# A hybrid decoder layer on eight cores: channel mixers cut by d_ff, and three tiles of them scheduled inside the token mixers

## The chip, the cores and the metric

One Trainium2 chip; the program runs on all 8 of its cores at once, each core on its own batch element, with no traffic between them. The metric is the device time of one execution, in microseconds (us), of the slowest core. Lower is better.

## The reference, cut to what matters

```python
def reference(x, mem, positions, ...):
    h = x                                                    # (8, 2048, 1024)
    h = h + 0.5 * _swiglu(_rmsnorm(h, ffn1_norm), wg1, wu1, wd1)    # D_FF = 2816
    h = h + _mixer(h, mem, positions, ...)
    h = h + 0.5 * _swiglu(_rmsnorm(h, ffn2_norm), wg2, wu2, wd2)
    return _rmsnorm(h, final_norm)

def _swiglu(x, wg, wu, wd):
    return (jax.nn.silu(x @ wg) * (x @ wu)) @ wd

def _mixer(...):
    z = _rmsnorm(h, mix_norm) @ w_in        # cq, ckv, krope, gq, gk, gv, ga, gr, xq, gz
    o_mla = _mla(...) @ mla_w_o             # 8 heads, causal, over all earlier tokens
    o_gla = _gla(...) @ gla_w_o             # 4 heads, a state carried along the sequence
    o_x = _cross(...) @ x_w_o               # 4 heads into 256 memory tokens
    gates = jax.nn.sigmoid(gz + gate_bias)  # three gates per channel
    return (gates[0] * o_mla + gates[1] * o_gla + gates[2] * o_x) @ w_out
```

The two `_swiglu` are the channel mixers, `_mixer` is the token mixer. The channel mixers work on each token alone; the token mixer of a token needs the tokens before it.

## The kernel before, in words

The 2048 tokens of a core are four tiles of 512 tokens (TT). Everything is kept transposed, channels on the 128 partitions and tokens along the free axis, so a matmul is 128x128 weights against 128x512 activations and fills one of the eight PSUM banks. All four tiles of the residual h lie in SBUF (`hS`, 4 x 8 pieces of 128x512 f32).

The program is written as a list of operations (`FW.add`), each with the engines that may run it, a cost, and its dependences from the tiles it reads and writes. `FW.schedule` (L172) then plays the list through: it keeps a clock for each engine, takes the operation that can start first, and among those that are ready on an engine the one that was written down first. The result is a fixed order on each engine; `emit` writes it out with semaphore waits. Which PSUM bank and which weight slot an operation uses is settled when it is written down, before the order is known: `bank` (L401) and `pair` (L407) go round fixed sets (PA banks 0 to 3 for attention scores, bank 4 for attention outputs, PQ banks 5 to 7 for the rest of the token mixer), and `slot_view` (L493) goes round six weight slots (`ring`) of 128x2048 bf16.

The stages stand one behind the other:

- Norm and first channel mixer for all four tiles (`ffn`, L601). It goes over d_ff in 11 groups of 256. For a group it loads three slots of weights (`wload`, L498: f32 in DRAM, cast to bf16 on the way, issued from GpSimd's queue), and for each tile does 4 banks of 8 matmuls for gate and up rows, then Silu on ScalarE and a product on VectorE; then `down` (L604) does 8 banks of 2 matmuls, and VectorE adds each bank to h, so h is read and written once per group and channel piece. Beside it `side1` (L985) issues small work: constants, rope tables, keys and values of the memory (`memory_kv`), and the conversion of the token mixer's 42 weight blocks from f32 to bf16 in DRAM (`convert`, L505, five per group, also from GpSimd's queue, which it shares with `wload`).
- Four token mixers, tile after tile (`mixer_tile`, L685): projections; attention over all tiles so far (the scores of two key blocks in a pair of banks, one Exp of 128x1024); between heads two "units" of the linear attention and cross attention (`fill`); then the merge, 12 steps of a gate projection (slot wz, 16 matmuls) and an output projection (slot wo, 8 matmuls); then w_out. Its weights come by `mload` (L509) from the bf16 copy, on SyncE's queue.
- Norm and second channel mixer for all four tiles, the final norm (`done2`, L1023), and the store.

The softmax here doesn't subtract the row's maximum and nothing guards it: scores larger than these inputs give would overflow.

## Time and profile before

| | us |
|---|---|
| three timed runs | 1950.38, 1957.6, 2092.74 |
| their median | 1957.6 |
| the profiled execution: span of the slowest core | 1966.7 |
| spans of its eight cores | 1937.1 to 1966.7 |
| TensorE (PE) busy in it | 1725.2 (88%) |
| VectorE (DVE) busy | 1014.5 (52%) |
| ScalarE (ACT) busy | 669.7 (34%) |

The profile follows one execution on its slowest core. Its span runs from the first instruction to the last and is the own time that is known of it; a timed run gives a device time, and the median of these lies 9 us below that span. "PE busy" counts matmuls as they stream; the granted clock (PEclk) says at what part of 2.4 GHz. The DMA share is the mean busy share of the core's 16 DMA engines.

### The profile page before, as it was taken

What the parts mean: (1) busy time and instruction counts of PE and PEld (TensorE: products, weight loads), DVE (VectorE), ACT (ScalarE), POOL (GpSimd) and SP (SyncE); (2) the same over time, 40 slices, a digit from 0 to 9 for tenths busy, and PEclk for the clock granted to TensorE, in tenths of its full rate; (3) what the DMA queues carried; (4) which work ended last, traced back from release to release, by engine and by line L of the source; (5) the groups of instructions that cost most, each with busy time, mean ns of one, the idle gap of its engine ahead of it and who ended that gap; (6) DMA issues with size and microseconds to landing.
All of it is one profiled execution on the core that took longest, in us unless ns stands there. A gap on an engine that the chain in (4) does not pass through costs nothing.

```text
span 1966.7 us, 23970 instructions; the slowest of 8 cores (1937.1 to 1966.7 us)
## 1 busy us (share of the span) xinstructions
PE 1725.2 (88%) x7714; PEld 773.3 (39%) x7868; DVE 1014.5 (52%) x1718; ACT 669.7 (34%) x1014; POOL 60.0 (3%) x119
## 2 busy tenths in 40 slices
PE   2999995999987689867997889968899999999995
PEld 0444443344434234423442334423344444444442
DVE  3767772554555334432444334532348555666567
ACT  3411111001125642556334862658543111111124
POOL 1000001000000000000000000000000000000000
PEclk9999997788989799987998999979999999999998
DMA  9388877245232035600462014312253211122104
GB/s 224 62 101 100 105 108 101 37 59 74 53 126 87 30 97 162 187 26 33 134 222 78 27 61 165 117 33 103 83 143 54 43 33 33 33 50 48 33 1 171
DMA packets 49512, 168.91 MB, mean 86 GB/s; under 512 B 6816, under 2 KB 9264, under 8 KB 48432
## 3 DMA queue, kind: packets, MB, share of 16 engines
q0 software_dynamic: 13424, 55.55, 20.2%
q1 hardware_dynamic: 35968, 111.81, 17.5%
q8 instruction: 69, 1.13, 0.2%
q14 instruction: 51, 0.42, 0.1%
HBM read 204.00 MB, written 35.39 MB: 122 GB/s over the span
## 4 chain that ended last, share of the span: by engine, by line
PE 80%; ACT 7%; DVE 5%; issue 4%; DMA 3%; SPq 0%; ACTq 0%; DVEq 0%; POOLq 0%
PE ps_all L433 80%; ACT sa L459 2%; DMA hS<-x 2%; ACT hS L459 2%; DMA ring<-f 1%; ACT sa L897 1%; DVE hS L471 1%; DVE ntm L471 1%; ACT L459 1%; DVE om L466 1%; DVE sb L466 1%; ACT sa L908 0%; DVE hS L466 0%; DVE og L471 0%; ACT hS L482 0%
## 5 line engine op out<-in xcount | busy, mean ns | idle before, releaser
L433 PE MATMUL ps_all<-B,ring 128*128 128x512 bf16 x2760 | 638.6, 388 | 23.0 <-DMA ring<-f 17.5
L471 DVE SCALAR_TENSOR_TENSOR hS<-ps_all,hS 128x512 f32<-128x512 f32 (+1 forms) x744 | 457.1, 682 | 41.9 <-PE ps_all L433 40.6
L433 PE MATMUL ps_all<-sb,ring 128*128 128x512 bf16 (+1 forms) x1787 | 427.0, 389 | 15.7 <-DVE sb L471 6.1
L433 PEld LDWEIGHTS ps_all<-B,ring 128*128 128x128 bf16 x2816 | 279.9, 100 | 369.2 <-issue 84.3
L459 ACT ACTIVATE sa<-ps_all 128x512 f32<-128x512 f32 (+2 forms) x256 | 145.1, 569 | 790.8 <-PE ps_all L433 758.8
L433 PE MATMUL ps_all<-ntm,ring 128*128 128x512 bf16 x1310 | 328.7, 396 | 32.1 <-DVE ntm L471 11.2
L466 DVE TENSOR_TENSOR sb<-sa,ps_all 128x512 bf16<-128x512 f32 x176 | 120.4, 687 | 361.5 <-PE ps_all L433 354.7
L433 PEld LDWEIGHTS ps_all<-sb,ring 128*128 128x128 bf16 x1824 | 182.5, 100 | 238.0 <-issue 51.4
L433 PEld LDWEIGHTS ps_all<-ntm,ring 128*128 128x128 bf16 x1344 | 133.8, 101 | 203.1 <-issue 63.0
L471 DVE SCALAR_TENSOR_TENSOR sa<-sa,ps_all 128x512 f32<-128x512 f32 x96 | 65.6, 687 | 132.1 <-PE ps_all L433 110.6
L433 PE MATMUL ps_all<-sb,B 128*128 128x512 bf16 (+3 forms) x313 | 91.8, 367 | 34.3 <-ACT sa L897 18.3
L433 PE MATMUL ps_all<-sa,va 128*128 128x512 bf16 (+3 forms) x315 | 104.3, 386 | 19.8 <-DVE om L466 18.8
L459 ACT ACTIVATE sa<-ps_all,hv 128x512 f32<-128x512 f32 x96 | 65.3, 686 | 164.8 <-PE ps_all L433 150.3
L897 ACT ACTIVATE sa<-ps_all 128x1024 bf16<-128x1024 f32 x96 | 95.2, 1022 | 24.2 <-PE ps_all L433 20.3
L459 ACT ACTIVATE sb<-hS 128x512 bf16<-128x512 f32 x128 | 75.0, 623 | 55.6 <-DMA hS<-x 25.6
L433 PE MATMUL ps_all<-sb,ones 128*128 128x512 bf16 (+1 forms) x151 | 52.1, 410 | 44.7 <-ACT sb L459 34.9
L163 POOL DMA_DIRECT2D ring<-f x66 | 35.4, 539 | 1700.3 <-PE ps_all L433 1625.0
L459 ACT ACT_TABLE_LOAD x39 | 50.0, 1283 | 55.8 <-PE ps_all L433 48.1
L466 DVE TENSOR_TENSOR sa<-sa,utri 128x128 bf16<-128x128 bf16 (+1 forms) x96 | 22.6, 246 | 79.5 <-ACT sa L908 49.7
L471 DVE SCALAR_TENSOR_TENSOR B<-hS,vecs_s,sa 128x512 bf16<-128x512 f32 x64 | 43.1, 747 | 34.4 <-ACT sa L459 34.4
L466 DVE TENSOR_TENSOR om<-ps_all,sa 64x512 bf16<-64x512 f32 x32 | 22.0, 687 | 73.9 <-ACT sa L459 64.6
L433 PEld LDWEIGHTS ps_all<-sb,B 128*128 128x128 bf16 x320 | 28.7, 101 | 79.1 <-issue 66.1
(99 smaller groups left out, 973.6 us busy)
## 6 DMA issues: line engine op xcount, KB each, us to landing
ring<-wb SPq DMA_DIRECT2D x112, 512.0 KB, 4.0
ring<-f POOLq DMA_DIRECT2D x66, 512.0 KB, 6.8
wb<-wm POOLq DMA_DIRECT2D x28, 512.0 KB, 17.2
ring<-wb SPq DMA_DIRECT2D x48, 256.0 KB, 3.7
hS<-x SPq DMA_DIRECT2D x16, 512.0 KB, 30.8
spill<-hS SPq DMA_DIRECT2D x4, 2048.0 KB, 8.9
hS<-spill SPq DMA_DIRECT2D x16, 512.0 KB, 5.7
outT<-hS SPq DMA_DIRECT2D x16, 512.0 KB, 2.8
```

Of the source, the lines that this page charges most:

```text
L163: op = self.add([(q, lambda e: e.dma_start(out=o, in_=i), 0.9 if q == "pool" else 0.06)], outs=[out, *outs], ins=[in_, *ins], waits=waits)
L433: i = e.matmul(_ap(o), lhsT=_ap(l), rhs=_ap(r), start=st, stop=sp)
L459: f.add([("act", lambda e: e.activation(out=_ap(out), in_=_ap(in_), func=func, scale=_ap(scale), **kw), c_act(out, bias is not None))], ou ...
L466: f.add([(eng, lambda e: e.tensor_tensor(out=_ap(out), in0=_ap(a), in1=_ap(b), op=op), c_dve(out, rate))], outs=[out], ins=[a, b, *extra_ins])
L471: f.add([("dve", lambda e: e.scalar_tensor_tensor(out=_ap(out), in0=_ap(in0), scalar=_ap(scalar), in1=_ap(in1), op0=op0, op1=op1), c_dve(o ...
L897: f.add([("act", lambda e, PT=PT, ap2=ap2: e.activation(out=PT.bf().ap.rearrange("p (a b) -> p a b", a=2), in_=ap2, func=AF.Exp, scale=SC) ...
```

## The change

What it does, part by part:

1. **Channel mixer, new form.** `ffn` goes over d_ff in parts of 5, 5, 4, 4, 4 blocks of 128 (8, 7, 7 for a single tile). In a part it makes all activations of the part (tiles `aT`), block by block: one slot holds gate and up weights of a block. Then it makes the part's down projection with 4 or 5 (8 or 7) matmuls into one bank, and VectorE adds that bank to h once per part. The matmuls are the same number.
2. **Order of the stages.** The first channel mixer runs for tiles 0, 1, 2 as a stage of its own ("ffn1a"; weights used by three tiles). Tile 3's is written as a stream with its order number raised by LATER (`f.base`), so that the planner takes from it only what no operation of the token mixers can use. The second channel mixer of tiles 0 and 1 are two more such streams. That of tiles 2 and 3 has a base too, but its slots belong to a later epoch, and it runs as the last stage ("ffn2b"). A stream of one tile loads all weights of its channel mixer anew, as f32 with the cast.
3. **Banks and slots bound at issue.** `Bank` objects have a kind; `schedule` gives them a free PSUM bank or one of seven ring slots when their first user is placed, within limits per kind (four banks for a stream, three slots for its weights, four slots for the token mixer's).
4. **Silu in the streams** is Tanh(x/2) and one more VectorE operation.
5. **h leaves SBUF.** There are three places for h tiles in place of four; the token mixer reads h piece by piece from DRAM, adds, writes back (two 256 KB transfers per piece), and the norms before and after read the pieces once more.
6. **Norm sums** of the token mixer's output and of the streams are added up by VectorE, with one matmul at the end in place of eight.
7. **Attention** uses single banks: an Exp of 128x512 per key block in place of one of 128x1024 per two. Copies may go to either engine. The rope rows are spread by two transfers in place of 16 per tile.
8. **Beginning.** x of tile 0 is loaded first, the first weights are tied behind parts of x, and the first 15 tile-blocks have a written order (OPENING). `convert` issues two blocks per 128 of d_ff. x of tile 3 is streamed in for its norm.
9. **The planner's constants**: 270 GB/s in place of 300 for a transfer, 1.6 us (SyncE) or 2.6 us (GpSimd) behind it, a DMA is not issued more than 4 us ahead of the backlog, ScalarE may put off an operation for the sake of the loaded table.

```diff
 class FW:
...
-    def schedule(self):
+    def schedule(self, places, limits):
...
+        def begin_at(op, t):
+
+            for b in op.opens:
+                if not empty[b.store] or not tokens[b.kind] or line[b.kind][-1] is not b or ahead.get(b.epoch - 1):
+                    return None
+                t = max(t, min(empty[b.store])[0], min(tokens[b.kind]))
+            return t
+
+        pri = [op.pri for op in ops]
...
             op = ops[s]
+            for b in op.opens:
+                spot = min(empty[b.store])
+                empty[b.store].remove(spot)
...
+                b.ap = places[b.store][b.place]
+                op.deps.update(spot[2])
...
+SPLIT = (5, 5, 4, 4, 4)
+WIDE = (8, 7, 7)
+NS = max(SPLIT)
+LATER = 1000000
...
+    limits = {"f": 8, "w": 4, "s": 3, "o": 1, "q": 2, "m": 6, "g": 1, "x": 2, "n": 2,
+              "rf": 7, "rw": 3, "rm": 4}
...
+    def ffn(w, xs, hs, kind, silu, landed, side, split=SPLIT, by_tile=False, keep=None, opening=None):
...
+                pg, pu = bank(kind), bank(kind)
+                for p, o in ((pg, 0), (pu, 8)):
+                    for k0 in (0, 4):
+                        mm([(p, wgu[j][:, o + k, :], xs[i][k], k == 0, k == 7) for k in range(k0, k0 + 4)])
+                th = F2.get()
+                if silu:
+                    actf(th, pg, AF.Silu)
+                else:
+                    actf(th, pg, AF.Tanh, scale=0.5)
+                    stt(th, th, 1.0, pg, ALU.add, ALU.mult)
+                tt(a[i][j], th, pu, ALU.mult)
...
+            for q, c2, i in order:
+                c = 2 * q + c2
+                py = bank(kind)
+                for js in (range(ns - 1), (ns - 1,)):
+                    mm([(py, wds[q][:, j, c2 * 128:(c2 + 1) * 128], a[i][j], j == 0, j == ns - 1) for j in js])
+                h = hslot[hs[i]][c]
+                stt(h, py, 0.5 if silu else 0.25, h, ALU.mult, ALU.add)
...
+                py = proj(w_, c2 * 128, 128, mT, bank("m"))
+                hc = M2.get()
+                f.dma("sp", hc, spT[t][c], nbytes=262144)
+                stt(hc, py, 0.5, hc, ALU.mult, ALU.add)
+                f.dma("sp", spT[t][c], hc, nbytes=262144)
+                sums.take(hc)
...
+        if j >= 1:
+            for i in (2 * j - 2, 2 * j - 1):
+                convert(i)
...
+    ffn(f1_d, [nB[0], nB[1], nB[2]], (0, 1, 2), "f", True, lambda i, c: sums[i].take(hslot[i][c]), side1, by_tile=True,
+        opening=OPENING)
...
+    f.base = LATER
+    sums_b = Squares(F2, F1)
+    ffn(f1_d, [nB[3]], (0,), "w", False, lambda i, c: sums_b.take(hslot[0][c]), lambda j: load_x(3, 0) if j == 0 else None, WIDE)
+    f.base = 0
...
+    for t in (0, 1):
+        f.base = (2 + t) * LATER
+        sums_f = Squares(F2, F1)
+        ffn(f2_d, [n2[t]], (t,), "w", False, lambda i, c: sums_f.take(hslot[t][c]),
+            lambda j: reload(t, t) if j == 0 else None, WIDE)
+        final(t, t, sums_f, "w")
```

## Rows read from the trace of the kernel before

**Rows 1.** Stage windows, core 0: busy (count) of PE, PEld, DVE, ACT, POOL; clock, DMA share, GB/s.

```profile
0.00:47.00 47.00, 11.97 (x24) 2.80 (x25) 15.41 (x43) 14.85 (x25) 5.10 (x13) 1.00 0.96 215
47.00:300.00 253.00, 249.00 (x1131) 112.40 (x1152) 185.55 (x307) 51.91 (x83) 21.35 (x42) 1.00 0.74 98
300.00:347.00 47.00, 23.33 (x114) 13.15 (x116) 9.55 (x19) 8.91 (x16) 5.21 (x10) 0.71 0.76 99
347.00:475.00 128.00, 126.98 (x475) 52.91 (x484) 62.80 (x102) 10.75 (x18) 8.31 (x16) 0.81 0.38 50
475.00:561.00 86.00, 85.58 (x389) 38.83 (x395) 49.57 (x81) 10.15 (x17) 2.61 (x5) 0.99 0.34 77
561.00:1457.00 896.00, 742.27 (x3384) 333.58 (x3449) 369.89 (x654) 467.07 (x684) 0.00 (x0) 0.91 0.31 100
1457.00:1920.00 463.00, 459.83 (x2098) 209.12 (x2140) 283.79 (x457) 82.64 (x134) 17.43 (x33) 1.00 0.22 39
1920.00:1967.00 47.00, 26.22 (x111) 10.52 (x110) 37.98 (x59) 23.44 (x37) 0.00 (x0) 0.79 0.45 179
```

**Rows 2.** Windows of core 3, a stretch of the last channel mixer.

```profile
1450.00:1900.00 450.00, 449.93 (x2086) 203.72 (x2085) 277.69 (x450) 73.69 (x118) 14.79 (x28) 1.00 0.21 35
```

**Rows 3.** Waits of the engines, whole span: who for whom, total, times, longest.

```profile
PE ps_all L433 <- DMA ring<-f: 17.5, 1, 17.5
```

**Rows 4.** Timeline of GpSimd's queue before that wait.

```profile
316.82 2.55 POOL L163 DMA_DIRECT2D wb<-wm  x5 [1.20 <-PE ps_all L433]
320.90 1.09 POOL L163 DMA_DIRECT2D ring<-f  x2 [1.53 <-PE ps_all L433]
```

**Rows 5.** Windows in the token mixers: an attention stretch of tile 3, a merge.

```profile
1300.00:1350.00 50.00, 39.45 (x174) 15.67 (x177) 14.59 (x33) 39.91 (x54) 0.00 (x0) 0.88 0.16 54
738.00:800.00 62.00, 59.08 (x281) 27.63 (x285) 25.64 (x38) 19.08 (x29) 0.00 (x0) 1.00 0.64 184
```

**Rows 6.** Waits of PE alone, 580 to 1455 us.

```profile
PE ps_all L433 <- ACT hS L459: 25.7, 24, 1.9
...
PE ps_all L433 <- ACT sa L897: 18.7, 27, 1.8
```

**Rows 7.** DMA, 1457 to 1920 us: a queue's share of 16 engines; issues, KB, us to landing.

```profile
q0 software_dynamic: 4752, 17.30, 21.5%
ring<-f POOLq DMA_DIRECT2D x33, 512.0 KB, 5.2
```

**Rows 8.** The same view, 47 to 347 us.

```profile
q0 software_dynamic: 4791, 25.93, 69.6%
wb<-wm POOLq DMA_DIRECT2D x24, 512.0 KB, 17.4
```

**Rows 9.** The same view, 561 to 1457 us.

```profile
q1 hardware_dynamic: 29423, 88.94, 30.6%
ring<-wb SPq DMA_DIRECT2D x109, 512.0 KB, 4.0
```

**Rows 10.** Groups of instructions on the page: count, busy, mean ns, idle before.

```profile
L471 DVE SCALAR_TENSOR_TENSOR hS<-ps_all,hS 128x512 f32<-128x512 f32 (+1 forms) x744 | 457.1, 682 | 41.9 <-PE ps_all L433 40.6
L897 ACT ACTIVATE sa<-ps_all 128x1024 bf16<-128x1024 f32 x96 | 95.2, 1022 | 24.2 <-PE ps_all L433 20.3
L459 ACT ACTIVATE sa<-ps_all 128x512 f32<-128x512 f32 (+2 forms) x256 | 145.1, 569 | 790.8 <-PE ps_all L433 758.8
```

**Rows 11.** Windows of cores 7 and 3 over one and the same stretch.

```profile
347.00:475.00 128.00, 128.00 (x489) 53.08 (x488) 62.45 (x102) 11.73 (x20) 8.32 (x16) 0.81 0.36 50
347.00:475.00 128.00, 128.00 (x592) 57.95 (x591) 76.00 (x123) 13.75 (x23) 10.93 (x21) 1.00 0.51 67
```

**Rows 12.** Timeline of VectorE: the end of the first norm, and the end of the program.

```profile
28.98 5.39 DVE L471 SCALAR_TENSOR_TENSOR B<-hS,vecs_s,sa 128x512 bf16<-128x512 f32 x8 [19.41 <-ACT sa L459]
1958.10 5.39 DVE L471 SCALAR_TENSOR_TENSOR hS<-hS,vecs_s,sa 128x512 f32<-128x512 f32 x8 [3.41 <-ACT sa L459]
```

More of the change, by code:

```diff
@@ L93, in __init__ @@
         self.marks = []
+        self.base = 0
+        self.loads = 0
+        self.span = 0.0
+        self.busy = {}
         self.handles = {"pe": nc.tensor, "act": nc.scalar, "dve": nc.vector, "pool": nc.gpsimd, "sp": nc.sync}
@@ L145, in add @@
         op.table = table
+        op.pri = self.base + seq
+        for t in {id(_t(x)): _t(x) for x in [*outs, *ins] if isinstance(_t(x), Bank)}.values():
+            if not t.users:
+                op.opens.append(t)
+            t.users.append(seq)
+            op.banks.append(t)
         self.ops.append(op)
@@ L183, in schedule @@
         dma_free = 0.0
-        table = None
+        table = {"none"}
         avail = {e: [] for e in COMPUTE}
@@ L238, in schedule, with emit @@
         self.span = max(op.end for op in ops)
-    def emit(self, outputs):
-        self.schedule()
+        self.busy = {e: sum(next(c for (x, _, c) in o.alts if x == e) for o in ops if o.eng == e) for e in COMPUTE}
+    def emit(self, outputs, places, limits):
+        self.schedule(places, limits)
         sems, counts, known = {}, {}, {}
@@ L702, in mixer_tile @@
+        rmsnorm(kvq[0:3], [vcol(V_QN + i) for i in range(3)], 384, cqn, banks="m")
+        M2.put(*kvq)
+        cp(ga_t, pk[0:16, :])
+        t1, t2, kr = M2.get(), M2.get(), M1.get()
         tt(t1[64:96, :], pk[64:96, :], CS[t][0:32, :], ALU.mult)
@@ L1033, in build_program @@
+    mixer_tile(3, nM[3], lambda: norm_from_dram(2, V_F2, n2[2]), quiet, lambda r: norm_from_dram(3, V_F2, n2[3], r))
+    epoch[0] = 3
+    f.mark("ffn2b")
+    f.base = 4 * LATER
+    sums_l = [Squares(M2, M1, "f") for _ in range(2)]
+    ffn(f2_d, [n2[2], n2[3]], (0, 1), "f", True, lambda i, c: sums_l[i].take(hslot[i][c]),
+        lambda j: [reload(2 + i, i) for i in range(2)] if j == 0 else None, by_tile=True)
+    for i in range(2):
+        final(i, 2 + i, sums_l[i], "f")
     f.mark("end")
-    f.emit(outputs)
+    f.emit(outputs, {"ps": psum, "ring": ring}, limits)
```

785 lines of the change are left out of this document (469 added, 316 removed).

## The prediction

> **What bounds the kernel now.** I read the windows by stage first. Both channel-mixer stages are TensorE streaming without a gap: 459.83 of 463 us busy in the second one at clock 1.00, 249.00 of 253 in the first [rows 1]. The pitch of a 128x512 matmul there is 449.93/2086 = 0.2157 us [rows 2]. Time is lost in five other places [rows 1]. The head: 47 us until the channel mixer starts, with 12 us of PE and DMA at 0.96. A stall in the first mixer: PE is busy 23.33 of 47 us at 300 to 347, the wait behind it is one of 17.5 us on a weight load [rows 3], and GpSimd's queue shows five conversions issued just ahead of two loads [rows 4]. Then 128 us at clock 0.81. The token mixers: 896 us with PE busy 742.27 at a mean clock of 0.91, so 742.27 x 0.91 = 675 us of work at full clock and 221 us lost, a quarter. The tail: 47 us with 26 of PE. In the token mixers no single wait explains the loss: the largest two in PE's own list sum to 44 us and are many short ones on ScalarE [rows 6]; in attention on tile 3 ScalarE is busy 39.91 of 50 us while PE has 39.45 at clock 0.88 [rows 5]. So the stage is a chain of short handovers with too little independent work beside it, and in these stretches the clock is also lower.
>
> **The work that stays.** Matmuls of the channel mixers: 22 blocks x (16 + 8) = 528 per tile and mixer, 8 x 528 = 4224, at 0.2157 us = 911 us, as before. The change can only alter how PE is filled. By stage: three tiles 342 us (1584 matmuls), three streams 342, the last two tiles 228. The token mixers keep 675 us less seven norms whose eight matmuls become one or nothing (7 x 8 x 0.2157 = 12): 663.
>
> **Head.** Before, x of the first tile shares the DMA with the other weights and 6 MB of other x; its norm ends with the eight operations from 28.98 us [rows 12], and the second tile's is waited for too. Now 2.1 MB of x come first; at 215 GB/s [rows 1] that is 10 us, some 3 us to start, and about 5 us of norm before the first eight matmuls flow. I take 18 us, bounds 14 and 29. From there the opening needs 6.3 MB of x and five weight slots while PE has 15 tile-blocks of 16 x 0.2157 = 52 us: 29 us of DMA for x and 5 x 3 to 5 us for the weights fit.
>
> **First stage, three tiles.** 342 us, memory keys and values 9 us, squares 24 x 0.2157 = 5: 356. The risk is DMA. A weight load costs 21.5% x 463 / 33 = 3.0 us of all engines [rows 7]. In the stretch with conversions the queue used 69.6% of 300 us = 209 us [rows 8] for 22 loads (66 us) and the equivalent of 27.5 full conversions, so a conversion costs 5.2 us. The stage needs 33 loads' worth (99), 35.5 full conversions (185), four memory weights (12), x of three tiles (29), tile 3's x twice (19), and some 5 of small things: 349 us of DMA in about 384. That is 91% where before it was 74 to 76% [rows 1], with two conversions of 5.2 us queued per 15.8 us of PE. The seven slots let loads run far ahead, so I take one 10 us stall; bounds 0 and 45 (before, 75% gave about 25 us). VectorE is relieved: h is touched 120 times here in place of once per group, 272 times in the whole program in place of 704 at 0.682 [rows 10], 295 us less. It was hidden behind PE (185.55 of 253 us, 0.73, at most [rows 1]), so it is worth nothing by itself.
>
> **Token mixers with streams.** PE work is 663 + 342 = 1005 us. Three checks that no other resource takes over. ScalarE: 467 us [rows 1], plus 192 single Exps at 0.569 for 96 pairs at 1.022, +11 [rows 10]; one more Exp per head and tile on the diagonal, 32 x 0.2 = 6; streams 66 Tanh and 24 squares at 0.6 = 54: 538, 49% of the stage. VectorE: 370, plus streams 3 x (44 x 0.68 + 24 x 0.68 + 13 x 0.7) = 166, plus norm sums and rereading 45: 581, 53%. DMA: the queue used 30.6% x 896 = 274 us for 88.94 MB, 3.1 us per MB [rows 9]; streams add 99 loads x 3.0 = 297, h through DRAM adds 34 MB = 105: 676 us, 62%. So PE is the bound if the planner has stream work whenever the mixers leave PE idle, and there are 221 us of holes against 342 us of stream. Order permits it: tile 3's stream needs only its norm, tile 0's second mixer is ready after the first token mixer, tile 1's after the second. The ScalarE-bound stretches of tile 3 [rows 5] lose some 10 of 50 us and a stream fills them at a cost of about one Tanh per 5 us.
>
> What is left of the loss? The new waits: each PE block now waits in a fixed order for a handover that was planned to arrive just then, with transfers the planner only estimates. A channel-mixer stage before lost 3.2 of 463 us, 0.7%, the token mixers 25% [rows 1]; the woven stage lies nearer the first since a third of its matmuls depend on nothing recent. I take 57 us (5 to 6%), bounds 20 and 150, and 10 us for the two seams (norm after ffn1a, reload and norm before ffn2b). Queues that the edits pass: each of SyncE's 64 h transfers for w_out waits on VectorE with later weight loads queued behind it, and GpSimd's conversions stand ahead of weight loads; both are in these two terms. VectorE's added stream operation stands ahead of the next attention mask, a 0.68 us delay that the streams cover.
>
> **Clock.** For 128 us core 7 ran 489 matmuls where core 3 ran 592 [rows 11]: clock 0.81, neither of the full nor half levels (2.4 and 1.2 GHz), worth 128 x 0.19 = 24 us, and the slowest core has it. It followed the stall. I keep 24 us once, bounds 0 and 75. The gain from the token mixers' 0.91 is already in their sum.
>
> **Tail.** 228 us for the last stage plus 4 us of final squares. Behind the last matmul: add 0.7, square 0.6, matmul, Ln and Exp, the eight scalings of 5.39 us [rows 12], store: 12 us. Before, the tail also held a gap of some 8 us.
>
> **Sum of the span.** 18 + 356 + 10 + 1005 + 57 + 10 + 24 + 228 + 4 + 12 = 1724 us, against 47 + 514 + 896 + 463 + 47 = 1967 before. The median of the runs is 1957.6/1966.7 = 0.9954 of that execution's span, so 1724 x 0.9954 = 1716 us. The 243 us come as: head 29, first mixer with its stall and slow clock 514 less (356 + 10 + 24) and less the fourth tile's 114 = 10, token mixers 896 + 114 + 228 (the work moved in) less (1005 + 57 + 10) = 166, second mixer and tail 463 + 47 less (228 + 4 + 12 + 228) = 38.
>
> **Rules that speak against it.** The same window on each core shows 0.81 on cores 0, 1, 6 and 7 and 1.00 on 2 to 5, and all eight streamed at 1.00 from 50 to 300 us and through the last stage [rows 1, 2, 11]. The Trainium skill (TensorE: Matmul & The Clock Gate, Part 1) says that dense matmuls on three cores of a die bring the whole die to 13/16 of the clock for as long as the load lasts. By that rule the denser program gains nothing; this trace disagrees with "whole die" and with "as long as it lasts", and agrees with the value 0.81. The Trainium skill (DMA: Bandwidth & Descriptors, Issuing engines are not separate DMA queues) also says that transfers from all queues interleave on the same 16 engines, so a stream's loads would slow the token mixer's; no row of before has both at once.
>
> **Rivals.**
> (a) *DMA sets the pace.* The merge takes a pair of slots (wz, wo) every 24 x 0.2157 = 5.2 us, with four slots in place of six; a load lands in 4.0 us [rows 9], but a stream load of 3.0 us beside it makes it about 7, against 6 to 7 us from the freeing of a slot to its next use. If each of the 48 pairs is late by 1.5 us, that is 72 us; with 25 us more in the first stage 1716 + 97 = 1813. For it: DMA was at 0.64 in a merge with nothing else going [rows 5]. Against: PE then did not wait, 59.08 of 62 us, and a planner that knows it is behind puts stream matmuls there.
> (b) *The streams are not woven*: bank limits, slots or in-order binding keep them behind the mixers. Then 884 us stay, 342 follow: 18 + 366 + 884 + 342 + 24 + 232 + 12 = 1878, x 0.9954 = 1869. Against: they have banks and slots of their own.
> (c) *Slower than before: the clock of 0.81 holds while PE is dense.* All PE work is 911 + 663 + 22 = 1596 us; at 0.81 it costs 0.23 more, 367 us, less the 24 already in: 1716 + 343 = 2059. It turns slower than before once more than about 265/0.23 = 1150 us, 72% of the work, runs so. For it: denser PE than ever on all cores. Against: 450 us at 1.00 [rows 2].
>
> **How the numbers follow.** Forecast 1660 to 1770: 0.67. (a) 1770 to 1840: 0.18. (b) up to 1890: 0.07. (c): 0.04. Below 1660 (all losses at their low bounds, 1634 x 0.9954 = 1627): 0.02, unforeseen losses above 1890 0.02. The range of 1655 to 1840 holds about 0.85 by these cases and takes in the bounds of the mixer term. 2% of 1957.6 is 39 us, about what a measurement can tell from no change; faster by more than that, below 1918: 0.93; within: 0.03; slower: 0.04.
>
> **What would show it.** Right: the first channel-mixer matmuls before 20 us; VectorE's additions to h at 272 in place of 704; PE at 95% or more at clock near 1.00 from 400 to 1430 us; the last stage starting near 1475 us; DMA at 0.6 to 0.7 in the middle and over 0.9 before 370. Wrong: waits of PE on `ring` loads that sum to over 60 us would be (a); PE under 85% in attention stretches followed by a long block of pure channel mixer before ffn2b would be (b); matmuls at 0.265 us pitch over several hundred us would be (c). A planner whose DMA estimate is off by a tenth in the 91% stretch is what I would suspect first.

## The result and the profile after

The changed kernel takes 1791.15 us in the median; its time over that of the kernel before is 0.9127, with a 95% interval of 0.9083 to 0.9171: faster by 8.7%. (Executions in which one die ran at a lower clock throughout are in this median, but in no ratio and in no other median below.) The forecast was 1716 us, range 1655 to 1840. The profiled execution has a span of 1781.9 us on its slowest core, core 2, where the sum gave 1724: 58 us more. Readings without a core named are of core 2.

The windows by stage, cut where the first channel-mixer matmuls begin (18.4), where VectorE starts on tile 0's input for the token mixer (439), and where the last long wait of TensorE ends (1450). Columns as in [rows 1].

```profile
18.40:98.00 79.60, 61.43 (x263) 26.46 (x264) 24.67 (x39) 26.44 (x40) 10.83 (x21) 0.89 0.72 128
98.00:300.00 202.00, 178.15 (x825) 81.88 (x824) 86.43 (x138) 33.96 (x60) 22.04 (x42) 0.93 0.91 139
300.00:439.00 139.00, 134.24 (x611) 59.61 (x609) 54.53 (x82) 34.36 (x54) 14.71 (x28) 0.99 0.66 117
439.00:1450.00 1011.00, 947.12 (x4650) 442.74 (x4651) 552.44 (x965) 570.18 (x909) 43.03 (x81) 0.97 0.63 161
1450.00:1782.00 332.00, 317.50 (x1459) 142.70 (x1457) 141.09 (x209) 57.26 (x91) 32.35 (x61) 0.98 0.57 107
```

Against [rows 1]: the token mixers had PE busy 83% at clock 0.91; the woven stage has 94% at 0.97, with two and a quarter of the three streams inside: 1197 of their 1584 matmuls, for 387 of the last stream still stand behind 1450, as a block ahead of the last stage (see the checks below). What stands out is the first stage: of its 421 us from 18.4 on PE is idle 18.2 + 23.8 + 4.8 = 46.8. The gaps there, and those at the seams between the token mixers and ahead of the last stage, stand in PE's timeline (start, length, operation, count, in brackets the idle time before it and what ended it):

```profile
18.38 9.86 PE L558 MATMUL ps_all<-B,ring 128*128 128x512 bf16 x36 [4.60 <-DVE B L596]
...
97.08 2.29 PE L558 MATMUL ps_all<-aF,ring 128*128 128x512 bf16 x5 [12.03 <-DVE aF L591]
...
298.00 1.44 PE L558 MATMUL ps_all<-ntm,ring 128*128 128x512 bf16 x3 [17.67 <-DVE hS L596]
...
884.68 12.79 PE L558 MATMUL ps_all<-ntm,ring 128*128 128x512 bf16 x48 [9.57 <-DMA ring<-wb]
...
1449.81 12.26 PE L558 MATMUL ps_all<-aF,ring 128*128 128x512 bf16 x50 [12.75 <-DVE aF L591]
```

Four of the five name VectorE (`B` is the normed input, here in the head; `aF` the product of gate and up rows, `hS` the residual), though VectorE is under half busy. Its own timeline shows what it was doing ahead of the last three of these:

```profile
94.08 0.42 DVE L608 CAST ma<-ma 64x512 f32<-64x512 int32 x1 [18.52 <-DMA ma<-posr]
...
96.25 0.69 DVE L591 TENSOR_TENSOR aF<-fa,ps_all 128x512 bf16<-128x512 f32 x1
...
296.50 0.75 DVE L596 SCALAR_TENSOR_TENSOR B<-ma,vecs_s 128x512 bf16<-128x512 f32 x1 [10.77 <-DMA ma<-x]
297.17 1.28 DVE L596 SCALAR_TENSOR_TENSOR hS<-ps_all,hS 128x512 f32<-128x512 f32 x2
...
1442.88 0.75 DVE L596 SCALAR_TENSOR_TENSOR B<-ma,vecs_s 128x512 bf16<-128x512 f32 x1 [12.94 <-DMA ma<-spill]
```

Each time VectorE stands at an operation of a side job (the rope table's positions, tile 3's norm, the norm ahead of the last stage) whose small read has not landed, and the operation that TensorE needs is queued behind it. PE's list of waits puts this under `aF` and `hS`. The waits on weight slots, which I had looked for, are shorter: with the two on channel-mixer weights (5.1 and 4.3) they sum to 26.9 us (waited for, us, times, longest):

```profile
PE ps_all L558 <- DVE aF L591: 26.6, 5, 12.8
...
PE ps_all L558 <- DVE hS L596: 17.7, 1, 17.7
PE ps_all L558 <- DMA ring<-wb: 17.5, 5, 9.6
```

The DMA view of 98 to 300 us shows what the reads stand beside: the queue of weight loads and conversions holds 80.7% of the engines, and a 256 KB read takes 11.7 us from issue to landing, a weight load 23.4, where one took 5.2 in the last stage of before [rows 7].

```profile
q0 software_dynamic: 4866, 22.69, 80.7%
...
ring<-f1g POOLq DMA_DIRECT2D x10, 512.0 KB, 23.4
ma<-x SPq DMA_DIRECT2D x16, 256.0 KB, 11.7
```

The cores differ. The same stage ends at 438 on core 2 and at 409 on core 4, whose PE loses 15.5, 4.7 and 4.0 us in it:

```profile
18.40:98.00 79.60, 64.08 (x273) 27.57 (x271) 27.76 (x45) 26.53 (x40) 10.81 (x21) 0.89 0.74 133
98.00:300.00 202.00, 197.32 (x941) 92.42 (x942) 91.47 (x145) 39.49 (x68) 25.51 (x49) 0.99 0.96 142
300.00:409.00 109.00, 104.99 (x482) 46.61 (x479) 43.89 (x65) 27.73 (x45) 10.97 (x21) 1.00 0.73 136
```

The hold of 8 to 12 us by the positions is on all eight cores; the one of 17.67 is on core 2, with 6.93 on core 3, and on no other.

From the page: VectorE's additions to h, 232 here and 40 more under the name `ntm`, and ScalarE's table loads.

```profile
L596 DVE SCALAR_TENSOR_TENSOR hS<-ps_all,hS 128x512 f32<-128x512 f32 x232 | 157.1, 689 | 91.1 <-PE ps_all L558 90.1
...
L584 ACT ACT_TABLE_LOAD x89 | 114.2, 1283 | 77.4 <-PE ps_all L558 69.1
```

### The profile page after: what moved, and what is told of

The parts are those of the page before. It is cut to its first block, busy times and chain, and to the rows that moved or that the text cites. A ratio compares the mean times of both kernels' runs of the same rounds, so it can differ in the third digit from the quotient of the medians.

```text
span 1781.9 us, 24307 instructions; the slowest of 8 cores (1749.2 to 1781.9 us)
## 1 busy us (share of the span) xinstructions
PE 1642.9 (92%) x7812; PEld 754.3 (42%) x7812; DVE 870.2 (49%) x1464; ACT 729.6 (41%) x1165; POOL 124.9 (7%) x240
## 4 chain that ended last, share of the span: by engine, by line
PE 80%; DMA 12%; DVE 3%; ACT 2%; issue 2%; SPq 1%; POOL 0%; DVEq 0%; ACTq 0%; POOLq 0%
PE ps_all L558 80%; DMA ring<-wb 3%; DMA spill<-ma 2%; DMA ma<-x 2%; DMA ring<-f1d 1%; DMA ma<-posr 1%; DMA ring<-f1g 1%; DMA ma<-spill 1%; ACT mb L584 1%; DVE hS L596 1%; DMA hS<-x 1%; ACT ma L584 1%; SPq L205 1%; DVE mb L591 0%; DVE ma L596 0%
## 5 line engine op out<-in xcount | busy, mean ns | idle before, releaser
L558 PE MATMUL ps_all<-ntm,ring 128*128 128x512 bf16 x2224 | 543.9, 388 | 38.3 <-DVE hS L596 17.7
L558 PE MATMUL ps_all<-B,ring 128*128 128x512 bf16 x2112 | 475.7, 382 | 15.7 <-DVE B L596 10.4
L558 PE MATMUL ps_all<-aF,ring 128*128 128x512 bf16 x1232 | 300.8, 386 | 31.3 <-DVE aF L591 24.8
L584 ACT ACTIVATE fa<-ps_all 128x512 f32<-128x512 f32 x176 | 105.0, 597 | 494.2 <-PE ps_all L558 493.7
L591 DVE TENSOR_TENSOR aF<-fa,ps_all 128x512 bf16<-128x512 f32 x154 | 105.6, 687 | 256.3 <-PE ps_all L558 225.6
L596 DVE SCALAR_TENSOR_TENSOR hS<-ps_all,hS 128x512 f32<-128x512 f32 x232 | 157.1, 689 | 91.1 <-PE ps_all L558 90.1
L558 PEld LDWEIGHTS ps_all<-aF,ring 128*128 128x128 bf16 x1232 | 121.3, 99 | 180.4 <-issue 48.8
L584 ACT ACTIVATE mb<-ps_all 128x512 bf16<-128x512 f32 (+1 forms) x304 | 162.2, 577 | 49.0 <-PE ps_all L558 47.4
L558 PE MATMUL ps_all<-mb,va 128*128 128x512 bf16 (+1 forms) x320 | 108.8, 347 | 2.0 <-DVE mb L591 1.0
L558 PE MATMUL ps_all<-mb,B 128*128 128x512 bf16 (+2 forms) x320 | 94.6, 347 | 2.6 <-ACT ma L584 1.5
## 6 DMA issues: line engine op xcount, KB each, us to landing
wb<-wm POOLq DMA_DIRECT2D x28, 512.0 KB, 14.1
```

Source lines behind the costliest of these rows:

```text
L558: i = e.matmul(_ap(o), lhsT=_ap(l), rhs=_ap(r), start=st, stop=sp)
L584: f.add([("act", lambda e: e.activation(out=_ap(out), in_=_ap(in_), func=func, scale=_ap(scale), **kw), c_act(out, bias is not None))], ou ...
L591: f.add([(eng, lambda e: e.tensor_tensor(out=_ap(out), in0=_ap(a), in1=_ap(b), op=op), c_dve(out, rate))], outs=[out], ins=[a, b, *extra_ins])
L596: f.add([("dve", lambda e: e.scalar_tensor_tensor(out=_ap(out), in0=_ap(in0), scalar=_ap(scalar), in1=_ap(in1), op0=op0, op1=op1), c_dve(o ...
```

## The experiments

Theory: TensorE is the bound, and what is missing against the forecast comes from VectorE's fixed order. An operation planned for the moment at which a side read should land stands ahead of what TensorE needs, and in a crowded DMA queue the read lands late. Rivals: the weight loads themselves set the pace; ScalarE and VectorE do; the weaving gave little and most of the gain is elsewhere. The changed kernel was run again as `control`: 1780.47 us, ratio 0.9079 (0.9027 to 0.9131). The kernel before falls into two groups of times, near 1944 and near 1963 us, on each chip, which is why many of the intervals are half a per cent wide on either side. On the chip of unwoven, few_conv, early_pos and thin_stream six of its seven times lie in the lower group, on control's two of six; that alone can lift the ratios of these four by 0.5% (10 us) over the others'. So I give the difference of the medians beside that of the ratios.

| kernel | median us | ratio (95%) | first stage ends, mean (cores) | from there to the end, mean | slowest core over the mean |
|---|---|---|---|---|---|
| changed | 1786.3 | 0.9127 (0.9083 to 0.9171) | 421 (409 to 438) | 1348 | 13 |
| control | 1780.47 | 0.9079 (0.9027 to 0.9131) | 421 (409 to 432) | 1342 | 12 |
| unwoven | 1858.79 | 0.9558 (0.9542 to 0.9575) | 425 (411 to 433) | 1419 | 10 |
| few_conv | 1767.79 | 0.9118 (0.905 to 0.9186) | 408 (403 to 413) | 1347 | 8 |
| early_pos | 1791.58 | 0.9198 (0.9163 to 0.9233) | 433 (429 to 437) | 1347 | 11 |
| thin_stream | 1742.83 | 0.8961 (0.8945 to 0.8977) | 430 (427 to 433) | 1309 | 3 |
| slow_plan | 1823.59 | 0.9303 (0.9246 to 0.936) | 442 (432 to 457) | 1369 | 18 |
| spread_conv | 1770.85 | 0.9051 (0.897 to 0.9131) | 411 (400 to 423) | 1342 | 12 |
| thin_parts | 1806.03 | 0.9206 (0.9143 to 0.9269) | 427 (423 to 429) | 1371 | 7 |
| late_side | 1777.97 | 0.9074 (0.9004 to 0.9144) | 408 (403 to 415) | 1362 | 9 |
| late_spread | 1776.69 | 0.9073 (0.9011 to 0.9134) | 400 (396 to 407) | 1368 | 10 |
| silu_streams | 1774.48 | 0.9077 (0.8976 to 0.9178) | 424 (414 to 435) | 1339 | 11 |
| late_ends | 1759.88 | 0.9014 (0.8961 to 0.9068) | 399 (397 to 405) | 1349 | 7 |

The last three columns are of the profiled execution: its slowest span is their sum. The end of the first stage is read as the start of VectorE's eight scalings of tile 0 for the token mixer, on each core, such as this one of the changed kernel on core 2:

```profile
438.25 5.38 DVE L596 SCALAR_TENSOR_TENSOR ntm<-hS,vecs_s,ma 128x512 bf16<-128x512 f32 x8
```

In control the wait of the same kind near 290 us falls on cores 1, 2 and 7, of 18.79, 14.66 and 18.06 us, and these three are its slowest, 1772 to 1774 us against 1747 to 1765. So on which cores the read of x is late differs from execution to execution, and the metric, the slowest core, pays it nearly whole. It also moves the mean: changed, control, silu_streams and thin_stream have the same order of VectorE there, the wait is on 1, 3, 3 and 8 of their cores, and the stage ends at 421, 421, 424 and 430 in the mean. A difference of under 10 us in that column shows nothing by itself, so I count the cores that have the wait too. The part behind it repeats within 6 us.

**unwoven.** The streams lose their low priority and are planned in the order in which they are written.

```diff
-LATER = 1000000
+LATER = 0
```

> Theory (weaving fills the holes of the token mixers, worth some 150 us): the streams now come in the order in which they were written, as solid blocks ahead of the token mixer that follows them, with no lower rank. The holes of the token mixers return where no stream stands beside them: a time between 1860 and 1960 us, windows in attention with TensorE under 85% busy, and the time at half clock up from about 100 us towards 190. Rival (the gain comes from the head, from the relief of VectorE and from the planner's binding of banks at issue, and a greedy planner fills holes in any order): within 25 us of the changed kernel, 1765 to 1815.

1858.79 us, just below the lower edge of what the theory gave. Against control the priority is worth 0.048 of 1958 us, 94 us, by the ratios (84 against the first measurement's) and 78 by the medians: about half of the total gain of 180. The other half does not need it; the early start, the shorter tail and the filling of holes that the planner does in any order are candidates, and no run parts them. In windows of 100 us from 430 to 1730, PE on core 2 is busy under 85% in four (from 430, 930, 1330 and 1530), in control in one (from 830). The longest waits are at the seams. In PE's timeline:

```profile
985.43 0.59 PE L558 MATMUL ps_all<-mb,ones 128*128 128x512 bf16 x1 [16.66 <-DVE mb L591]
...
1587.70 9.54 PE L558 MATMUL ps_all<-mb,ring 128*128 128x512 bf16 x32 [13.39 <-DMA ring<-wb]
```

**few_conv.** Only 4 of the 42 conversions of the token mixers' weights are done; the mixers read those four blocks over and over, so their weights are not the reference's.

```diff
     def convert(i):
+        if i >= 4:
+            return
...
-        f.dma("sp", t[:, 0:n], wb_T[b][:, 0:n], nbytes=128 * n * 2)
+        f.dma("sp", t[:, 0:n], wb_T[b % 4][:, 0:n], nbytes=128 * n * 2)
```

> Only the first four of the 42 blocks of the token mixer's weights are converted, and all of its loads read those four; so its weights are not the reference's, and the instructions on the four compute engines are the same in number. Theory (the first stage lost 41 us against the forecast because the DMA queue is over 90% full there, and operations on VectorE that wait for a side transfer hold up the products and additions that TensorE waits for): the waits of 12 us at 97, 5 us at 212 and 18 us at 298 go, and the start of the token mixer comes 25 to 40 us earlier; total 1735 to 1765 us. Rival (these waits come from the planned order itself or from the opening, not from the load on the DMA): total within 10 us of the changed kernel.

The first stage ends 13 us earlier in the mean, not 25 to 40, and the wait near 290 is gone from all eight cores, where early_pos and thin_stream on the same chip have it on all eight; the DMA share from 98 to 300 is 0.45 in place of 0.91. The rest of the program takes the same time. The three executions took 1763.55, 1767.79 and 1787.36 us, 13 us under control in the median, and the ratio's interval covers both no gain and 15 us. The hold by the positions stays (7.9 to 11.7 us), and so does the longest wait, ahead of the last stage (15.94 in control; this and the next kernels' gaps are core 2's). So the conversions are needed for the hold near 290. For the one near 97 the run can't tell: the four conversions that it keeps are those around the read of the positions, issued at 68.5 to 70.8 us, the read at 69.4.

```profile
91.46 2.29 PE L558 MATMUL ps_all<-aF,ring 128*128 128x512 bf16 x5 [8.30 <-DVE aF L591]
...
1412.16 13.17 PE L558 MATMUL ps_all<-aF,ring 128*128 128x512 bf16 x50 [18.79 <-DVE aF L591]
```

**spread_conv.** All conversions are kept: 31 in the first stage, thinned to three per two blocks, and 11 between the heads of the first token mixer.

```diff
+NC = 31
...
-            for i in (2 * j - 2, 2 * j - 1):
+            for i in range(3 * (j - 1) // 2, min(NC, 3 * j // 2)):
                 convert(i)
...
             M1.put(qh[hh])
+            if t == 0:
+                for i in late_convert[2 * hh:2 * hh + 2]:
+                    convert(i)
             fill(2)
```

> 31 of the 42 conversions are issued in the first stage, 3 per two blocks, and the last 11 between the heads of the first token mixer. Theory (the share of the DMA over 90% in the first stage is what makes the side transfers late): the share falls to about 0.8, the waits before 300 us shrink by 15 to 25 us, and the time by 10 to 20 us against the control. Rival (as few_conv has hinted, where 38 conversions less took less than expected): the first stage's waits shrink but come back at the seams, the time the same within 8 us.

6 us under control by the ratios and 10 by the medians, within the interval. The DMA share from 98 to 300 falls to 0.82, the hold by the positions to at most 8.3 us (7.8 to 11.9 in control). The stage ends at 400 to 410 on five cores and at 421 to 423 on the three that still have the wait near 290, of 12 to 16 us; 9 us earlier in the mean, and what comes later is unchanged. So thinning the conversions shortens both holds and removes neither.

**thin_stream.** A stream's weight load brings only the first eighth of its slot; the plan is untouched. The streams compute with stale weights.

```diff
+        m = n // 8 if kind == "rw" else n
-        op = f.dma("pool", t[:, 0:n], src[:, 0:n], ...
+        op = f.dma("pool", t[:, 0:m], src[:, 0:m], ...
```

> The three streams load only the first eighth of each weight slot, and compute with what lies in the rest; the planned order is the same. Theory (in the woven stage DMA is not what TensorE waits for, save at the seams between tiles, where loads of the token mixer's weights land late): 5 to 20 us less, at the waits of 5 and 10 us for token mixer weights near 650 and 885 us. Rival (a) of the prediction (the streams' loads slow those of the token mixer all along): 40 to 90 us less. A third case, in which the loads' engines are not shared in a way that matters: no change.

1742.83 us: 23 us below control by the ratios, 38 by the medians. The first stage is no shorter, since no stream runs there; from there to the end it is 1309 us against 1342, the only kernel of which that part is shorter by over 10. The wait at 872 and the one for a load behind it (10.08 and 6.26 in control) are 4.93 and 7.02 here, and the one of 15.94 near 1440 is gone. On every core the waits of over 4.5 us behind the first stage sum to 17 to 20 us, in control to 42 to 57.

```profile
288.32 1.44 PE L558 MATMUL ps_all<-ntm,ring 128*128 128x512 bf16 x3 [16.95 <-DVE hS L596]
...
863.80 11.96 PE L558 MATMUL ps_all<-ntm,ring 128*128 128x512 bf16 x48 [7.02 <-DMA ring<-wb]
```

So the streams' transfers beside the token mixers' cost about 23 to 38 us (33 by the table's column), more than the theory's 5 to 20 and less than the rival's 40 to 90. Rival (a)'s mechanism exists, at under half of the 72 us that it gave the token mixers, and at the seams, not in each pair of the merge.

**early_pos.** The first two tiles' positions are loaded at the very start.

```diff
+    pos_pre = [M2.get(), M2.get()]
+    for t in range(2):
+        f.dma("sp", pos_pre[t].i32()[64:128, :], ...)
     x1 = load_x(1, 1)
```

> The positions for the first two tiles' rope tables are loaded at the start, ahead of the x of tile 1, in place of beside the conversions. Theory (the 12 us wait of TensorE at 97 us is a cast on VectorE that waits 18.5 us for the 128 KB of positions, with the product for TensorE queued behind it): that wait falls to under 4 us and the whole is 6 to 12 us faster, 1771 to 1779 us. Rival (the DMA queue was behind there anyway, so that TensorE waits for a weight load in its place): the wait moves to a weight load and the time is the same within 4 us.

The wait of 12 us at 97 is gone and one of the same kind of size has come behind it:

```profile
113.55 4.00 PE L558 MATMUL ps_all<-aF,ring 128*128 128x512 bf16 x9 [8.36 <-DMA ring<-f1d]
```

The new wait, 8.4 to 12.8 us, is on all eight cores. Here the rival was right: once VectorE no longer stalls at 97, TensorE runs into the weight queue, which is behind at that point anyway. The whole is 11 us above control by the medians, but that is not shown to be the edit's doing: the stage ends 12 us later in the mean with the wait near 290, of 16 to 21 us, on all eight cores, as in thin_stream on the same chip, whose stage ends at 430 against 433 here. There is no gain, and a loss is open.

**slow_plan.** The planner takes every transfer for slower: 215 GB/s in place of 270, and 2.2 and 3.6 us of latency in place of 1.6 and 2.6.

```diff
-                dma_free = begin + op.nbytes / 270e3
-                end = dma_free + (1.6 if op.hw else 2.6)
+                dma_free = begin + op.nbytes / 215e3
+                end = dma_free + (2.2 if op.hw else 3.6)
```

> The planner reckons with 215 GB/s in place of 270 for a transfer and with 2.2 and 3.6 us behind it in place of 1.6 and 2.6. Theory (the waits that are left come from side transfers that land later than planned, with in-order VectorE and SyncE held up): the waits at 97, 212 and 298 us and at the seams shrink by half, 15 to 35 us less than the control. Rival (the DMA is simply full in the first stage, and a planner that knows it can do nothing): within 8 us of the control. A third case: the planner now holds back loads that would have been in time, and the time rises by 10 to 40 us.

0.0224 above control, 44 us: 21 in the first stage and 27 behind it, the third case. The hold of VectorE by x is gone; the one by the positions is not, and costs TensorE 5.1 to 9.7 us in place of 7.8 to 11.9 (VectorE's timeline, first line below). In the first stage TensorE now waits for loads that the plan issues late, and so it does at every seam:

```profile
92.44 0.42 DVE L608 CAST ma<-ma 64x512 f32<-64x512 int32 x1 [13.88 <-DMA ma<-posr]
...
290.53 3.15 PE L558 MATMUL ps_all<-aF,ring 128*128 128x512 bf16 x7 [12.64 <-DMA ring<-f1d]
...
896.04 4.42 PE L558 MATMUL ps_all<-ntm,ring 128*128 128x512 bf16 x10 [17.84 <-DMA ring<-wb]
...
1476.42 0.59 PE L558 MATMUL ps_all<-mb,ones 128*128 128x512 bf16 x1 [20.76 <-DVE mb L591]
```

A planner that is told the truth on average is not what is missing; the bandwidth figure also decides when it starts loads.

**thin_parts.** d_ff is cut into nine parts in place of five, with more additions to h and more, smaller loads.

```diff
-SPLIT = (5, 5, 4, 4, 4)
+SPLIT = (5, 2, 2, 2, 2, 2, 2, 2, 3)
```

> The two stages of their own go over d_ff in parts of 5, then seven of 2 and one of 3 blocks, in place of 5, 5, 4, 4, 4, so that VectorE adds to h 9 times per piece in place of 5, some 160 additions or 110 us of VectorE more, in stages where it was 50% busy. Theory (the relief of VectorE was hidden behind TensorE): within 10 us of the control. Rival (the relief is a main source of the gain): 30 us or more above it.

0.0127 above control, 25 us, between the theory's 10 and the rival's 30, and nearly all of it behind the first stage (1371 against 1342). VectorE is busy 950 us in place of 870. The waits ahead of tile 1 and of the last stage are over 20 us each (5.37 and 15.94 in control):

```profile
654.90 5.55 PE L558 MATMUL ps_all<-ntm,ring 128*128 128x512 bf16 x13 [20.21 <-DMA ring<-wb]
...
1456.18 15.48 PE L558 MATMUL ps_all<-aF,ring 128*128 128x512 bf16 x64 [20.28 <-DVE aF L591]
```

Whether it is VectorE's additions or the smaller loads that lengthen them, this run can't tell, since it changes both.

**late_side.** The planner's estimate stays, but for the reads that feed side jobs of VectorE, which it now takes to land 12 us later.

```diff
+SIDE = 12.0
...
-                end = dma_free + (1.6 if op.hw else 2.6)
+                end = dma_free + (1.6 if op.hw else 2.6) + op.late
...
-            f.dma("sp", b, src(c), nbytes=262144, after=after)
+            f.dma("sp", b, src(c), nbytes=262144, after=after, late=SIDE)
```

> The planner is told that the position loads and the reads of x and of the spilled stream into ma land 12 us later than it thinks; all else in its estimate stays, and no work is added or removed. Theory (VectorE runs in order, and the operation planned for such a read's arrival holds the additions and products that TensorE needs): it plans other VectorE work ahead of those operations, so the waits of 12 us at 98, of 17.7 at 298 and of 13 to 16 before the last stage shrink by half or more; 1745 to 1768 us, ratio 0.890 to 0.902 against the changed kernel's 0.908 to 0.913. Rival (the DMA queue is behind there whatever the order is, as where the positions were loaded early): the same microseconds come back as waits for weights or for the token mixers' seams, within 8 us of the changed kernel or slower, ratio 0.905 to 0.925.

Both were half right. The waits of 11.69 at 97, 14.66 at 291 and 15.94 at 1441 of control are gone, and the first stage ends 12 us earlier in the mean, 17 on the slowest core. Near 290 no core waits, with the DMA share from 98 to 300 still at 0.93: there it was the order on VectorE that made TensorE wait. Near 97 it only hid another wait: as in early_pos, 8.3 to 12.7 us for a weight load come behind it, on all eight cores. And the part behind the stage is 20 us longer, and the time is that of control. PE's timeline shows the waits that have come:

```profile
115.13 3.49 PE L560 MATMUL ps_all<-aF,ring 128*128 128x512 bf16 x9 [10.05 <-DMA ring<-f1d]
...
863.83 0.59 PE L560 MATMUL ps_all<-mb,ones 128*128 128x512 bf16 x1 [12.97 <-DVE mb L593]
...
1140.42 0.59 PE L560 MATMUL ps_all<-mb,ones 128*128 128x512 bf16 x1 [12.22 <-DVE mb L593]
...
1466.24 5.28 PE L560 MATMUL ps_all<-ntm,ring 128*128 128x512 bf16 x16 [13.09 <-DVE fa L598]
```

Tile 1's projections start 24 us ahead of control's (621 against 645); the square sum that ends tile 2 is 11 us behind (1140 against 1129). So it is lost between the token mixers, where this edit plans the norms late too.

**late_spread.** The same with spread_conv's conversions.

> The same, with the conversions of the token mixers' weights thinned out in the first stage as in spread_conv (31 there, 11 in the first token mixer). If the two are separate causes (order on VectorE, and pressure on the DMA engines in the first 300 us) their gains add: 8 us less than late_side. If there is one cause, within 4 us of late_side. If the rival holds for late_side, this is at the spread_conv level, ratio 0.905.

The gains add in the first stage, another 8 us, which ends at 396 to 407 on all cores: the wait for a weight load near 110 is 4.2 us at most, and from 45 us on none over 6 us is left in the stage on any core. The part behind it is again long, 1368, and the time is that of late_side.

**silu_streams.** The three woven tiles take Silu in place of Tanh and of the operation on VectorE that goes with it.

```diff
-    ffn(f1_d, [nB[3]], (0,), "w", False, ...
+    ffn(f1_d, [nB[3]], (0,), "w", True, ...
...
-        ffn(f2_d, [n2[t]], (t,), "w", False, ...
+        ffn(f2_d, [n2[t]], (t,), "w", True, ...
```

> The four woven channel-mixer tiles take Silu instead of Tanh with its added multiply: VectorE has about 88 operations of 0.69 us (60 us) less, ScalarE changes its table more often between Silu and Exp. Theory (TensorE is the bound in the middle, the other engines matter only where an operation in order is late): within 8 us of the changed kernel, ratio 0.903 to 0.917, though ScalarE's table loads go from 89 to over 120. Rival (ScalarE's and VectorE's queues carry the seams): over 15 us off in one direction, slower if the table loads decide, faster if VectorE's 60 us do.

Within 6 us of control by the medians and 0.0002 by the ratios, with VectorE 44 us less busy (825), ScalarE 21 us more (750) and 104 table loads in place of 89. (I had counted four woven tiles and 60 us; there are three, 66 operations.) Neither engine's total load sets the time.

**late_ends.** The late landing is kept for the first stage and the norm ahead of the last stage, and taken from the norms and rope tables between token mixers; conversions as in spread_conv; the last stage opens with four units of tile 2, whose input is ready.

```diff
+OPENING2 = [(0, 0), (1, 0), (2, 0), (3, 0), (0, 1), (1, 1), (2, 1), (3, 1), (4, 0), (4, 1)]
...
-            f.dma("sp", b, src(c), nbytes=262144, after=after)
+            f.dma("sp", b, src(c), nbytes=262144, after=after, late=late)
...
-    mixer_tile(3, nM[3], lambda: norm_from_dram(2, V_F2, n2[2]), quiet, lambda r: norm_from_dram(3, V_F2, n2[3], r))
+    mixer_tile(3, nM[3], lambda: norm_from_dram(2, V_F2, n2[2]), quiet, lambda r: norm_from_dram(3, V_F2, n2[3], r, SIDE))
...
-        lambda j: [reload(2 + i, i) for i in range(2)] if j == 0 else None, by_tile=True)
+        lambda j: [reload(2 + i, i) for i in range(2)] if j == 0 else None, by_tile=True,
+        opening=OPENING2)
```

> The corrected landing (12 us later) stays only where TensorE has other work to be given: the position loads and the reads of x in the first stage, and the norm ahead of the last stage; the norms between token mixers are planned as in the changed kernel. The last stage opens with four units of tile 2 (whose input is ready) before the first of tile 3, and the conversions are thinned out. Theory (where TensorE is given independent work the hold of VectorE costs nothing, and at the seams of the token mixers there is none to give): the first stage ends about 20 us earlier as in late_side (14.6 us more PE work done by 430) and keeps it, the waits of 5 to 13 and 13 to 16 before the last stage fall below 6 in sum; 1745 to 1762 us, ratio 0.890 to 0.900. Rival (the order in front of each seam is set by the DMA reads behind it, so what is won ahead of a seam is waited off at it, as in late_side and few_conv): 1770 to 1785, ratio 0.903 to 0.911, with waits at the seams near 640, 870 and 1130 that sum to over 35 us against the 25 to 30 of the changed kernel.

1759.88 us, the lowest of the kernels that compute the reference: 21 us under control in the median, 0.0065 (13 us) in the ratio, on another chip and with intervals that overlap. Its times, 1755.8 to 1766.4, lie all below control's 1775.2 to 1783.5. The table says how: the first stage 22 us shorter, the cores closer together, and the part behind it back at 1349, so late_side's 20 us were in the main what it planned late between the mixers: the norms there, and the rope tables of tiles 2 and 3. The time is at the upper edge of what the theory gave, the ratio just past it, and the waits at the seams have not shrunk (36 to 55 us in sum, control 42 to 57). The opening order could not help: what waits there is the last stream, which stands ahead of the last stage as in the changed kernel, and the hold has moved to its additions to h, again behind the norm's reads. In the timelines of PE and then of VectorE:

```profile
1417.66 1.01 PE L562 MATMUL ps_all<-ntm,ring 128*128 128x512 bf16 x2 [14.22 <-DVE hS L600]
```

```profile
1405.33 0.75 DVE L600 SCALAR_TENSOR_TENSOR B<-ma,vecs_s 128x512 bf16<-128x512 f32 x1 [13.01 <-DMA ma<-spill]
...
1416.16 0.75 DVE L600 SCALAR_TENSOR_TENSOR B<-ma,vecs_s 128x512 bf16<-128x512 f32 x1 [6.95 <-DMA ma<-spill]
1416.83 1.28 DVE L600 SCALAR_TENSOR_TENSOR hS<-ps_all,hS 128x512 f32<-128x512 f32 x2
```

## Why the prediction was right, and where its sum fell short

**Right: what the change does and its sign.** The token mixers lost a quarter to short handovers, and independent matmuls fill that. PE's total of busy time is 1642.9 us against 1596 of work forecast at full clock. Unwoven shows that the low priority carries about half of the gain.

**The step that failed: "so I take one 10 us stall; bounds 0 and 45".** Against the forecast by stage:

| | forecast | core 2 | mean of the cores |
|---|---|---|---|
| head and first stage | 18 + 356 + 10 = 384 | 438 | 421 |
| the rest, clock term in it | 1005 + 57 + 10 + 24 + 228 + 4 + 12 = 1340 | 1343 | 1348 |
| span | 1724 | 1781.9 | 1769 |

Of the 58 us, 54 are in the first stage of the slowest core: 37 more of idle time (46.8, past the bound of 45) and 18 more of busy time (374 against 356). Of these 18 some 14 are the lower clock (0.94 in the mean) and 4 work that I had counted low: the stage runs 1624 matmuls of full width (350 us at 0.2157) and 72 of half the width (9.6 us busy). I had worked out DMA at 91% there; it is 0.91 from 98 to 300 and 0.79 over the whole stage. And I suspected a planner that is off.

What I had wrong is the path by which a late transfer reaches TensorE. I priced the one that before showed, a wait on a weight slot [rows 3]. Here it is a small read of a side job, waited for by VectorE, with TensorE's work behind it: 12.03 + 17.67 of the idle time on this core. I named this kind of queueing for SyncE and GpSimd only; of VectorE I wrote that its added operation costs "a 0.68 us delay".

For the 17.67 the runs show it: such a wait is on 1 to 8 cores of each kernel that leaves that part of the stage alone, and on none where those reads are planned to land later (late_side), with all conversions there, nor where the conversions are gone (few_conv), though there too the eight scalings of that norm stand ahead of 14 additions to h (of 12 in the changed kernel). (Thin_parts, which plans the stage anew, has none either.)

For the 12.03 it is half of the account. VectorE's hold is what ends that wait, but without the hold TensorE waits 8.3 to 12.8 us for a weight load (early_pos, late_side), on the path that I had priced; only with the conversions thinned as well are both gone (late_spread). One of the two remedies ends the stage 9 to 13 us earlier in the mean, both together (late_spread, late_ends) 20 to 22, at 396 on the best core, 12 us from the 384 of the sum. And it was a sum for one core where the metric takes the worst of eight: 13 us between the slowest and the mean had no term.

**The mixer term was right in size.** Idle time past 439 us is 63.9 + 14.5 = 78.4 against 57 + 10 + 12. The clock term, 24, measured 1264.6 busy less 1237 of work, 28. The two could be off against each other, as the 675 us of mixer work was itself taken from a mean clock. In the profile before I had also read the two largest waits of [rows 6] as one behind the other: between them in PE's list stands one of 19.9 us on VectorE (`om`), so that not only ScalarE's handovers made up the loss. And the low bounds of the terms sum to 1649, not 1634; nothing else was worked out from it.

**The checks.** First matmuls before 20 us: 18.38. Additions to h 272: 232 + 40. DMA over 0.9 before 370: from 98 to 300; 0.6 to 0.7 in the middle: 0.63. PE at 95% near 1.00 from 400 to 1430: 94.6% at 0.98. The last stage near 1475: missed. Its first gate and up rows (input `B`) run at 1534 on core 2:

```profile
1534.43 2.75 PE L558 MATMUL ps_all<-B,ring 128*128 128x512 bf16 x12
```

1459 matmuls remain at 1450 where the last stage and its squares need 1072, so 387 of the last stream, 84 us, were left over and run as a solid block in between. TensorE being busy in it, the sum doesn't change; but it is the sign of rival (b), in small, and it means that in the token mixers the planner placed less of the stream than I had counted on.

**The rivals.** (a) DMA as the pace: waits of PE on slots sum to under 30 us, not over 60, but thin_stream finds 23 to 38 us at the seams, against 72 for the token mixers in this rival. (b) Not woven: 1869 forecast; the nearest experiment, which still weaves in written order, gave 1859. (c) The clock of 0.81 held while PE is dense: no. Core 0, which had 0.81 in [rows 1], streams in the last stage of the changed kernel at full clock:

```profile
1600.00:1700.00 100.00, 99.53 (x456) 45.38 (x464) 41.03 (x60) 10.53 (x18) 10.04 (x19) 1.00 0.48 78
```

The rule of the Trainium skill (TensorE: Matmul & The Clock Gate, Part 1), that a dense load on three cores holds the die at 13/16, does not describe the profiled execution: PE is denser on all eight cores than before, with mean clocks of 0.958 to 0.976. With the rule of the Trainium skill that transfers of all queues share the same engines (DMA: Bandwidth & Descriptors, Issuing engines are not separate DMA queues) these runs agree: `ring<-wb`, from SyncE's queue, lands in 4.4 us with streams beside it where it took 4.0 [rows 9], and thinning the loads of GpSimd's queue (thin_stream) took it back to 4.0 from 439 to 1430 us and PE's waits on it from 16.0 to 7.9 us on core 2.

## What to carry to other kernels

When work is moved into an ordered program, list for every engine what stands behind each operation that waits for a transfer, not only for the queue that issues it. A half-idle VectorE held TensorE for 30 us in the first stage of the slowest core. Then ask what stands behind such a hold: without it, the 12 us at 97 came back as a wait of 8 to 13 us for weights, until the queue was thinned too. A planned order is as good as its latest small transfer: correct the landing of those reads alone, where the DMA is crowded and other work can go first; making all transfers slower in the plan cost 44 us. And where the metric is the slowest of several cores, read the stage on each of them: a wait that two or three cores draw costs as much as one that all have.

## What the runs showed of the hardware

Around the wait that ends at 298 us the granted clock is 0.50 (1.2 GHz) in the last 8 us of the gap and in the first 4 us of matmuls behind it, and 0.97 in the next 4; the loss behind a gap of 17.7 us is about 2 us (10 matmuls where 20 fit).

```profile
290.00:298.00 8.00, 0.00 (x0) 0.03 (x1) 1.50 (x3) 0.00 (x0) 0.00 (x0) 0.50 0.80 133
298.00:302.00 4.00, 4.00 (x10) 1.48 (x11) 4.00 (x8) 0.00 (x0) 0.00 (x0) 0.50 0.70 131
302.00:306.00 4.00, 4.00 (x20) 1.75 (x18) 2.72 (x5) 0.00 (x0) 0.00 (x0) 0.97 0.00 1
```

I had not expected how unevenly a crowded DMA serves its users: in the same 202 us a 256 KB read from SyncE's queue took 11.7 us and a 512 KB conversion 14.1, but a weight load 23.4, though the loads and the conversions come from one queue.
